# Value projections of an unnormalised residual, scaled per token at the copy out

## The reference, cut to what matters

```python
h = x                                    # the residual that the first block returns: x + y @ w_out
def rms_norm(x, g):
    y = x * rsqrt(mean(x * x, axis=-1) + 1e-6)
    return y * g
xn = rms_norm(h, norm1_g)
proj = xn @ w_in                         # queries, keys, values of 8 "fox" heads, 8 forget logits,
                                         # queries, keys, values of 8 dilated heads
```

## Time and profile before

| | |
|---|---|
| median of 3 runs | 2270.02 us (2269.95 to 2271.81) |
| profiled execution: its time | 2269.04 us |
| profiled execution: its span | 2267.2 us |
| PE busy | 2210.5 us, 97% of the span |
| DVE, ACT, POOL busy | 1304.5, 902.4, 1244.4 us |
| mean granted clock | 0.995 |

### The profile page before, as it was taken

One profiled execution on the slowest core, in us unless ns is written; L12 is line 12 of the kernel. 1 busy time (PEld: TensorE's weight loads), 2 busy tenths in 40 slices (PEclk: granted clock), 3 DMA queues, 4 the chain that ended last, 5 costly groups with the idle time before them and its releaser, 6 DMA issues.

```text
span 2267.2 us, 29807 instructions
## 1 busy us (share of the span) xinstructions
PE 2210.5 (97%) x9694; PEld 1736.1 (77%) x9694; DVE 1304.5 (58%) x2401; ACT 902.4 (40%) x1429; POOL 1244.4 (55%) x824
## 2 busy tenths in 40 slices
PE   8999999999999998999999999999999999999998
PEld 5666665777777776788888888888887888888886
DVE  5454332225643685797676665222223988888887
ACT  4565544335544554434323333222222433333333
POOL 3432022244434332268888888888886655555553
PEclk9999999999999999999999999999999999999999
DMA  7664233325423221245666666666656999999996
GB/s 244 200 212 150 79 89 125 90 92 171 149 75 103 76 85 47 93 94 90 147 144 148 140 147 145 144 148 127 113 105 190 351 325 358 349 356 350 353 356 241
DMA packets 240050, 396.96 MB, mean 175 GB/s; under 512 B 87992, under 2 KB 162744, under 8 KB 239712
## 3 DMA queue, kind: packets, MB, share of 16 engines
q1 hardware_dynamic: 161088, 328.48, 44.6%
q0 software_dynamic: 78880, 67.50, 14.9%
HBM read 330.60 MB, written 61.01 MB: 173 GB/s over the span
## 4 chain that ended last, share of the span: by engine, by line
PE 58%; DVE 2%; ACT 0%; DMA 0%; issue 0%; SPq 0%; DVEq 0%; ACTq 0%
PE bank L1474 30%; PE bank L1485 23%; PE bank L1230 4%; PE bank L1457 0%; ACT staged L1525 0%; DMA tail<-gates 0%; DVE u_split L2278 0%; DVE low L1966 0%; DVE tail L2210 0%; DVE tail L2245 0%; DVE tail L2243 0%; DVE tail L2246 0%; DVE tail L2189 0%; DVE staged L2192 0%; DVE tail L2199 0%
## 5 line engine op out<-in xcount | busy, mean ns | idle before, releaser
L1107 POOL DMA_INDIRECT gates<-low x384 | 627.9, 1635 | 140.3 <-issue 116.8
L1474 PE MATMUL bank<-h_high,u_tiles_split 128*128 128x512 f32 x2048 | 630.9, 389 | 2.2 <-DVE u_tiles_split L2177 2.2
L1075 POOL TENSOR_TENSOR u_split<-blocks,u_split 128x1024 fp32r<-128x1024 f32 (+1 forms) x102 | 245.2, 2404 | 586.7 <-ACT u_split L1629 558.0
L1230 PE MATMUL bank<-h_high,u_split 128*128 128x512 f32 x1664 | 540.5, 400 | 10.8 <-POOL u_split L1075 6.8
L1485 PE MATMUL bank<-v_split,a_split 128*128 128x512 f32 x2286 | 520.2, 390 | 2.8 <-DVE a_split L2317 2.8
L1485 PEld LDWEIGHTS bank<-v_split,a_split 128*128 128x128 f32 x2286 | 430.1, 188 | 92.9 <-DVE v_split L2314 3.1
L1474 PEld LDWEIGHTS bank<-h_high,u_tiles_split 128*128 128x128 f32 x2048 | 384.6, 188 | 81.9 <-issue 2.4
L1474 PE MATMUL bank<-h_low,u_tiles_split 128*128 128x512 f32 x1024 | 398.6, 389 | 0.0
L1230 PEld LDWEIGHTS bank<-h_high,u_split 128*128 128x128 f32 x1664 | 313.7, 189 | 86.6 <-issue 21.3
L2177 DVE TENSOR_TENSOR u_tiles_split<-tail,u_tiles_split 128x1024 fp32r<-128x1024 f32 x128 | 157.1, 1228 | 361.5 <-ACT u_tiles_split L1816 360.6
L1230 PE MATMUL bank<-h_low,u_split 128*128 128x512 f32 (+1 forms) x704 | 274.4, 390 | 0.0
(11 more groups left out here) (232 smaller groups left out, 2360.9 us busy)
## 6 DMA issues: line engine op xcount, KB each, us to landing
tail<-in_uT SPq DMA_DIRECT2D x128, 512.0 KB, 3.8
tail<-in_v SPq DMA_DIRECT2D x128, 512.0 KB, 5.4
gates<-blocks SPq DMA_DIRECT2D x32, 768.0 KB, 5.8
tail<-gates SPq DMA_DIRECT2D x128, 192.0 KB, 5.6
kept_hidden<-tail SPq DMA_DIRECT2D x96, 192.0 KB, 1.9
tail<-kept_hidden SPq DMA_DIRECT2D x96, 192.0 KB, 5.7
blocks<-in_r SPq DMA_DIRECT2D x24, 512.0 KB, 4.0
blocks<-in_conv SPq DMA_DIRECT2D x16, 512.0 KB, 4.4
```

What stands on the lines that cost most here:

```text
L1075: nc.gpsimd.tensor_tensor(flat(u, 1)[:, 0:n], ring[:, loads[0] % NW, 0:n], flat(u, 0)[:, 0:n].bitcast(F32), ALU.subtract).then_inc(s_wlo, 1)
L1107: nc.gpsimd.indirect_dma_start(gate_elements, bass.IndirectOffsetOnAxis(ap=expert_no[tb][:, k:k + 1], axis=0), expert_gate[tb][:, k:k + 1] ...
L1230: last = mm(ps[0:m, :], flat(u, part)[:, k * m:(k + 1) * m], x, start=(k == 0 and j == 0), stop=(k == nk - 1 and j == 2))
L1474: last = mm(bank[slot % 2][:, :], U4[:, slot, w, k, :], x[:, k, :], start=(k == 0 and x is hh and w == 0), stop=(k == KD - 1 and w == 1))
```

## The change: what it does

In the loop over the output projections, DVE now also makes a high part `x * g` (`early_high`, a `tensor_scalar` into the new buffer `x2_parts`) and a low part (`early_low`, a `scalar_tensor_tensor` that subtracts the high part) of each finished residual tile. The projections `v2` 0 to 3 read these in place of `hh` and `hl`. `v2` 0 stands ahead of the norm, `v2` 1 to 3 behind it, and the forget projection comes behind all four, in one piece. The norm's TensorE part gets eight small float32 matmuls with two columns each (the sums of squares again, with the tokens along the partitions, into the other `ax` bank) and loses the three matmuls on constants; ACT waits for the eight before its Ln, and has an Ln and an Exp more of 128x8 numbers. The copy out of the four fox value banks moves from ACT to DVE, where it is a `tensor_scalar` with the token's root. The rest, forget projection, dilated values, queries and keys, uses the normalised tiles as before.

```diff
     for f in range(KD):
         post("res", f, [tile("wo", f, KD, P, True)])
+        STEPS.append(("early_high", "x2", f))
+        STEPS.append(("early_low", "x2", f))
         STEPS.append(("square", "x2", f))
         if 0 < f < KD - 1:
             STEPS.append(("sum", "x2", f))
-    STEPS.append(("norm", "x2"))
-    STEPS.append(("high_h", "x2"))
-    forget = len(PROJ) + 1
-    part(forget, 0, 2)
-    tile("v2", 0, 2, T)
+    for i in range(4):
+        tile("v2", i, 2, T)
+        if i == 0:
+            STEPS.append(("norm", "x2"))
+            STEPS.append(("high_h", "x2"))
+    STEPS.append(("scaled_values",))
     post("forget", 0, [tile("wf", 0, KD, 8, True)])
-    for i in range(1, 8):
+    for i in range(4, 8):
         tile("v2", i, 2, T)
...
+        def early_high(key, k):
+            return (oh[0] if key != "x2" else o_parts)[:, k, :]
+        def early_low(key, k):
+            return hl[:, k, :] if key == "h2" else (KA if key == "x" else QA)[:, k, :] if k < 4 else \
+                (oh[1] if key == "x" else KA)[:, k - 4, :]
...
                     for tb in range(TB):
                         if i == 4:
-                            if tb < TB - 1:
-                                pe.wait_ge(s_vfree, tb + 1)
-                            else:
-                                pe.wait_ge(s_evac, ev(pi[("v2", 3)]))
+                            pe.wait_ge(s_vfree, tb + 1)
                         for k in range(2):
                             t = 2 * c + k
+                            high, low = hh[:, t, :], hl[:, t, :]
                             if i < 4:
-                                pe.wait_ge(s_hl, parts0["x2"] + t + 1)
+                                pe.wait_ge(s_early_low, early_no("x2", t))
+                                high, low = early_high("x2", t), early_low("x2", t)
...
                     mm(ax[i % 2][:, :], ones, sq[:, j % NQ, :], start=False, stop=True).then_inc(s_aux, 1)
+                    if key in ("x2", ):
+                        for tb in range(TB):
+                            to, tokens = ax[(i + 1) % 2][:, 2 * tb:2 * tb + 2], slice(tb * P, (tb + 1) * P)
+                            mm(to, rs[:, tokens], ones[:, 0:2], start=True, stop=False)
+                            last = mm(to, sq[:, j % NQ, tokens], ones[:, 0:2], start=False, stop=True)
+                        last.then_inc(s_tok, 1)
...
-                    keep_busy(i, 3)
+                    if key not in EARLY_PHASES:
+                        keep_busy(i, 3)
...
                 if kind == "v2":
-                    if i % 4 == 3:
+                    if i == 7:
...
+                if key == "x2":
+                    act.wait_ge(s_tok, 1)
                 A(r, ax[i % 2][0:rows, 0:N], ACT.Ln, ...)
                 A(r, r, ACT.Exp, scale=-0.5).then_inc(s_rs, 1)
+                if key in ("x2", ):
+                    A(rinv[:, 0:2 * TB], ax[(i + 1) % 2][:, 0:2 * TB], ACT.Ln, bias=col("eps")).then_inc(s_tokrs, 1)
+                    A(rinv[:, 0:2 * TB], rinv[:, 0:2 * TB], ACT.Exp, scale=-0.5).then_inc(s_tokrs, 1)
...
+            def early_parts(key, k, low):
+                if not low:
+                    dve.wait_ge(s_post, post_no[({"x2": "res", "h2": "res2"}[key], k)])
+                    V.tensor_scalar(early_high(key, k), x, g, None, ALU.mult).then_inc(s_early_high, 1)
+                    return
+                dve.wait_ge(s_early_high, early_no(key, k))
+                V.scalar_tensor_tensor(early_low(key, k), x, g, early_high(key, k).bitcast(F32),
+                                       ALU.mult, ALU.subtract).then_inc(s_early_low, 1)
+            def scaled_values():
+                dve.wait_ge(s_tokrs, 2)
+                for tb in range(TB):
+                    if tb < TB - 1:
+                        dve.wait_ge(s_vb, tb + 1)
+                    else:
+                        dve.wait_ge(s_proj, pi[("v2", 3)] + 1)
+                    V.tensor_scalar(VA[:, tb].rearrange("p h d -> p (h d)"), bank[3 + tb][:, :],
+                                    rinv[:, 2 * tb:2 * tb + 1], None, ALU.mult).then_inc(s_vfree, 1)
```

More of the change, by code:

```diff
@@ L599, in program @@
         PT_odd = region(HH + 6144, 4 * T, 4)
+        o_parts = place("x2_parts", oT_off, [8, T], F32R)
         QB = place("queries_high", q2_off, [4, T], F32R)
@@ L749, in program @@
         pi = {(k, i): n for n, (k, i, _) in enumerate(PROJ)}
-        evacuated = [not (kind == "v2" and i % 4 < 3) for kind, i, _ in PROJ]
+        evacuated = [not (kind == "v2" and i != 7) for kind, i, _ in PROJ]
         def ev(n):
@@ L835, in program, with early_no, wait_evacuated, roots @@
         H_NO = {"x": 0, "x2": 1, "h2": 2}
+        EARLY_PHASES = ("x2", )
+        def early_high(key, k):
[3 more added lines that the diff above has]
+                (oh[1] if key == "x" else KA)[:, k - 4, :]
+        def early_no(key, k):
+            return KD * EARLY_PHASES.index(key) + k + 1
+        scaled_no = {}
+        for s in STEPS:
+            if s[0] == "scaled":
+                scaled_no[s[1]] = len(scaled_no) + 1
+        def wait_evacuated(eng, n):
+            if n in scaled_no:
+                eng.wait_ge(s_scaled, scaled_no[n])
+            else:
+                eng.wait_ge(s_evac, ev(n))
+        def roots(key):
+            return rs
         parts0 = {key: sum(n for _, n in PHASES[:i]) for i, (key, _) in enumerate(PHASES)}
@@ L1222, in split @@
                     first = i < 3 if kind == "br" else i == 0
+                    early = {}.get(kind)
                     x_low = {"br": ol, "wo": yl, "wo2": ol}.get(kind, hl)
@@ L1228, in split @@
                         high = oh[t // 8][:, t % 8, :] if kind == "br" else hh[:, t, :]
-                        for j, (part, x) in enumerate(((0, high), (0, x_low[:, t, :]), (1, high))):
+                        low = x_low[:, t, :]
+                        if early:
+                            high, low = early_high(early, t), early_low(early, t)
+                            if kind == "wq" and i == 0:
+                                pe.wait_ge(s_early_low, early_no("h2", t))
+                        for j, (part, x) in enumerate(((0, high), (0, low), (1, high))):
                             last = mm(ps[0:m, :], flat(u, part)[:, k * m:(k + 1) * m], x,
@@ L1691, in norm @@
                     act.wait_ge(s_norm, j - 1)
-                r = rs[0:rows, 0:N]
+                r = roots(key)[0:rows, 0:N]
                 if key == "x":
                     act.wait_ge(s_par, 16)
+                if key == "x2":
+                    act.wait_ge(s_tok, 1)
                 A(r, ax[i % 2][0:rows, 0:N], ACT.Ln, bias=col("eps", 0, 0, rows),
@@ L1933, in norm @@
                 dve.wait_ge(s_rs, j)
-                r = rs[0:rows, 0:N]
-                for k in range(nk):
+                r = roots(key)[0:rows, 0:N]
+                for k in ks or range(nk):
                     if key == "x":
@@ L1973, in norm @@
                 if key in H_NO:
-                    low_h(key, KD - 1)
+                    if k == KD - 1:
+                        low_h(key, KD - 1)
                 else:
@@ L2144, in _ @@
                     settle()
-                if s[0] == "norm":
+                if s[0] == "norm" and s[1] in ():
+                    pass
+                elif s[0] == "norm":
                     norm(s[1])
+                elif s[0] == "normalise":
+                    norm(s[1], range(s[2], s[3]))
+                elif s[0] in ("early_high", "early_low"):
+                    early_parts(s[1], s[2], s[0] == "early_low")
+                elif s[0] == "scaled":
+                    scaled(s[1])
+                elif s[0] == "scaled_values":
+                    scaled_values()
                 elif s[0] == "split":
```

44 lines of the change are left out of this document (37 added, 7 removed).

## The result

| | before | changed |
|---|---|---|
| median beside each other, 12 executions each | 2271.77 us | 2277.14 us |
| ratio, 95% interval | | 1.0018 (1.0010 to 1.0027) |
| profiled execution: time, span | 2269.04, 2267.2 us | 2274.18, 2272.4 us |

The changed kernel is slower by 0.1 to 0.27% in this set. The same kernel was timed twice more beside the kernel before, with ratios of 1.0005 (0.9997 to 1.0014) and 1.0014 (1.0005 to 1.0023). So the size is about 0.1%, 1 to 4 us. One of the changed kernel's 12 executions took 2783.59 us at a mean granted clock of 0.751; the ratio leaves it out, and without it the median is 2277.12. The median of 2277.14 lies 1.5 us above the top of the predicted range; those of the two later sets, 2273.89 and 2274.89, lie inside it.

A forecast was written before the change was run, and what follows sets the result against it. PE, busy 97% of 2267.2 us, was taken as the bound, so only gaps between its matmuls matter. A shift of +0.06 us plus 1.5 for the clock gave +1.6: 2271.6 us, no measurable change, range 2265.4 to 2275.6.

The forecast's parts named there:

- Clock: At PE's new wait ahead of the fourth value projection: granted clock falls, costing 1.5 us, bounds 0 and 2.5.
- The base: Time of the kernel before that the forecast was added to: median of the runs, 2270.02 us.
- PE's gain: At the norm: PE pays 3.44 us in place of 7.79, a gain of 4.35 us.
- ACT takes it back: ACT casts the fourth value projection's weights only behind the norm and eight roundings; PE waits 4.41 us.
- the first rival: No wait ahead of the fourth value projection; PE keeps 4.35 us, time 2265.7 us; chance 0.12.
- Work costed at nothing: Behind the norm and in the output projections: DVE's copies and early parts, later forget chain, all covered by PE's projections.
- The third rival: POOL is late in the output projections behind DVE's early parts; 4.7 us over seven periods, 2276.3 us; chance 0.07.
- I found none there: Behind 697 us: no later wait with another cause than PE, so a shift carries to the end as it is.
- the example: PE's earlier wait of 3.46 us for POOL at 884.72, where the clock fell to 1.2 GHz, 1.7 us lost.
- The sum's upper end: Whole kernel: dearest bounds of the main course, +4.3 us, against a forecast of +1.6; main course's chance 0.78.

The follow-up runs named there:

- Moving the cast: Changed kernel with ScalarE's weight cast for the fourth value projection behind the fourth rounding, not the eighth; ratio 0.9974 to the kernel before, 2267.87 us.
- wait filled: Changed kernel with four float32 matmuls on constants in the wait ahead of the fourth value projection; ratio 0.9996 to the kernel before, 2270.97 us.
- four small matmuls: Changed kernel with four in place of eight small matmuls, those adding the summed squares left out; stage to the first query projection 57.34 us.
- with it filled: Changed kernel with four matmuls on constants ahead of the fourth value projection and three ahead of the third query projection; ratio 0.9998 to the kernel before, 2270.41 us.
- early parts: Kernel before with DVE's early high and low parts made in the output projections and read by nobody; norm to first query projection 56.68 us.
- shifted: Kernel before with seven in place of three matmuls on constants behind this norm; ratio 1.0000 to the kernel before, 2272.19 us.
- half filled: Changed kernel with two matmuls on constants in the wait ahead of the fourth value projection, 2.05 us left idle; one execution took 2276.06 us.

## Why the prediction was wrong

Nearly every step of it held. The step that failed is "Clock": one fall for 1.5 us, 2.5 at most, and nothing at the waits behind. The base, three executions, was off too.

- *PE's gain.* The first value projection starts without a gap, and the small matmuls cost 1.70 us (647.66 to 649.36) for 1.74 taken. The third value projection ends 19.85 us behind the start for 19.76. Right.
- *ACT takes it back.* The fourth value projection starts 23.81 us behind the first; the prediction has 24.17 (665.00 - 640.83). Of the 0.36, the chain from Ln to cast gives 0.16 (11.13 for 11.29), POOL to PE 0.12 (2.44 for 2.56), Ln's start 0.07 and POOL's 0.01. The wait is 3.80 us behind the end of the last record; counted as in the prediction, from when the array is free (660.12 + 0.23), it is 3.96 for 4.41. Moving the cast took the wait away and gave 4.27 us against the kernel before, where the first rival had 4.35. Shown.
- *Work costed at nothing* (the copy out by DVE, the forget projection's later place, the early parts). With the wait filled the stage is 56.65 us, by the sum it should be 56.85 + 0.06 - 0.36 = 56.55. Right.
- *The third rival* did not come true: POOL started during `early_high`, took 2.54 us, and the next DVE operation waited. The Trainium skill's rule ("SBUF — State Buffer", Who interferes with whom: the first to issue keeps the shared ports for its whole instruction) agrees with the 2.76 us, and that it works out in POOL's favour was told by the earlier trace rows.
- *The clock* is the term that was mis-sized: +1.5 us with 2.5 as bound, from one earlier fall. It was 2.92 us at this wait (wait filled against not; 1.55 with four small matmuls), and the prediction had nothing for the waits behind. A fall behind the 3.3 us wait was in all three profiles of the changed kernel, 1.8 us (188.82 against 187.04, and 187.09 with it filled), and in none of those of the kernel before, with early parts, or shifted. Together 4.7 us, in place of 1.5. In the profile that is most of the 5.2 us between the spans. "I found none there" was said of waits with another cause than PE; that an old wait can get dearer I had not priced.
- *A dearer fall was in the trace already.* The prediction took its price from the fall at 884.72 alone. Near 853 the same trace has waits of 2.62 and 1.76 us (starts at 853.35 and 856.23), each shorter than the example with no fall, and behind them (0.14 + 0.50 + 0.05) x 5 = 3.5 us were lost, twice the example. Some 0.9 of it lie inside the second wait (1.76 us at half clock), which leaves about 2.5, the prediction's upper bound, where it took 1.5:

```profile
850.00:855.00 5.00, 1.56 (x5) 0.65 (x5) 4.88 (x12) 3.29 (x7) 0.00 (x0) 0.86 0.00 0
855.00:860.00 5.00, 3.77 (x9) 2.61 (x10) 4.69 (x17) 3.06 (x8) 0.00 (x0) 0.50 0.01 3
860.00:865.00 5.00, 5.00 (x31) 3.27 (x30) 4.34 (x16) 2.81 (x7) 0.00 (x0) 0.95 0.02 3
```

- *The base.* 2270.02 was the median of three executions. The kernel before had a median of 2271.77 over the twelve executions beside the changed kernel, and of 2272.70, 2273.06 and 2270.57 in the later sets, and single executions from 2268.7 to 2277.1. The sum's upper end, +4.3 us, stands for 2274.3, and the range went to 2275.6, so only 1.3 us were left for this, and the prediction gives no source for them. The sets resolved more than it had thought: their intervals are about 0.09% to each side, 2 us, and not 0.2%. Of the 7.1 us between 2270.02 and 2277.14, 1.75 are base (2271.77 - 2270.02) and 5.4 the pair's difference, where 1.6 was forecast.

The small loss was forecast the right way, and its size not: the forecast's +1.6 us lies within the interval of the second set (0.9997 to 1.0014), near the lower edge of the third and below the first. That the medians of the two later sets lie inside the range and the first one above it is the spread between sets, and not a better or worse forecast of the mechanism.

Open is why the clock falls behind the 3.3 us wait in the changed kernel and not in the kernel before. The wait has the same length (3.29 to 3.33) in all. It doesn't need the fall before it (half filled), and a shift of 1.5 us alone did not bring it (shifted). With the first wait wholly filled it did not come either. The profiles differ there in the moment of the wait and in what ran ahead of it, and which of these decides is not shown; the fall near 1036, which comes in four runs of thirteen, is open in the same way.

## What to carry to other kernels

When work is put ahead of a barrier to cover it, look at what else stands behind the barrier in the other engines' lists: here the cover lasted two projections, and the weights for the next were cast by the same ScalarE that did the norm. Moving one cast by four places turned +0.1% into -0.26%. And a wait of TensorE costs its length and the clock behind it: 3.8 us idle cost 2.9 us more in the changed kernel and 1.5 with four small matmuls. So price both, take the price from all falls in the trace and not from the wait that looks most alike, allow for a fall at old waits behind, and keep a margin of the kernel's own spread in a range of absolute time.

## What was not expected of the hardware

An idle stretch of 3.8 us let the clock go to 1.2 GHz in all three profiles of the changed kernel and with four small matmuls, and one of 3.3 us did so in some kernels and not in others. In one profile 2.05 us left it at 1.00, but that is no safe length: behind 2.17 us near 1036 it fell in four runs of thirteen. Counted over stretches of 5 us, every fall in the thirteen profiles but those in the last 15 us of the program lost about 1.7 or about 3.4 us of full speed, and the same wait brought either: 3.4 and 1.7 behind the 3.8 us, 1.7 and 3.4 behind the 3.3 us. A float32 matmul with two columns costs as much as one with 128: 0.106 us a record against 0.109.
